# Who makes the low half of each weight chunk, who adds up the last tiles at a norm, and where modulation rows are summed, in a 4-layer fp32 transformer kernel

## The reference, cut to what matters

```python
for l in range(2):                                    # first block
    mod = silu(c) @ w_ada[l] + b_ada[l]               # 9 rows of 1024: sh1, sc1, g1, ...
    y = swiglu(x * (1 + sc1) + sh1, ffn1 weights)     # 1024 -> 2816 -> 1024
    x = layer_norm(ALPHA * x + 0.5 * (1 + g1) * y)
    y = token_mixer(x * (1 + sc2) + sh2)              # w_in, retention/dilated/stick-breaking, w_out
    x = layer_norm(ALPHA * x + (1 + g2) * y)
    y = swiglu(x * (1 + sc3) + sh3, ffn2 weights)
    x = layer_norm(ALPHA * x + 0.5 * (1 + g3) * y)

for i in range(2):                                    # second block
    x = x + mixer_i(rmsnorm(x, g_mix[i]))             # i = 0: even mixer, i = 1: odd mixer
    x = x + cross_attn(rmsnorm(x, g_xattn[i]), rmsnorm(mem, g_mem[i]))
    x = x + square(relu(rmsnorm(x, g_mlp[i]) @ w_up)) @ w_down     # 1024 -> 4096 -> 1024
```

## Time and profile before

| | before |
|---|---|
| median of three runs | 3832.0 us |
| the profiled execution | 3830.17 us, span 3828.9 us |
| TensorE matmuls busy | 3560.9 us, 93% of the span |
| VectorE busy | 1763.9 us, 46% |
| ScalarE busy | 1220.7 us, 32% |
| GpSimd busy | 1426.8 us, 37% |
| mean granted TensorE clock | 0.954 of full speed |

### The profile page before, as it was taken

One profiled execution on the slowest core, in us unless ns is written; L12 is line 12 of the kernel. 1 busy time (PEld: TensorE's weight loads), 2 busy tenths in 40 slices (PEclk: granted clock), 3 DMA queues, 4 the chain that ended last, 5 costly groups with the idle time before them and its releaser, 6 DMA issues.

```text
span 3828.9 us, 41108 instructions
## 1 busy us (share of the span) xinstructions
PE 3560.9 (93%) x16548; PEld 2879.4 (75%) x16548; DVE 1763.9 (46%) x3102; ACT 1220.7 (32%) x1650; POOL 1426.8 (37%) x721
## 2 busy tenths in 40 slices
PE   8999899899998999899799988988989998988999
PEld 7888667688877888667678866746868886777888
DVE  4444654654455444644531235685552224564222
ACT  2222362332223222542332223235342232343222
POOL 3343432333344334322343342212344444525443
PEclk9999899899998999898899989978999998999999
DMA  6333321133342444211122221100212222222222
GB/s 252 143 145 134 107 88 66 72 120 139 143 143 99 143 144 142 99 66 45 65 89 95 92 83 55 56 12 34 89 59 95 99 99 71 98 69 84 91 98 77
DMA packets 52609, 373.42 MB, mean 98 GB/s; under 512 B 5826, under 2 KB 5954, under 8 KB 9539
## 3 DMA queue, kind: packets, MB, share of 16 engines
q1 hardware_dynamic: 52418, 370.79, 26.9%
HBM read 368.67 MB, written 2.10 MB: 97 GB/s over the span
## 4 chain that ended last, share of the span: by engine, by line
PE 82%; DVE 11%; ACT 3%; issue 2%; POOL 2%; DMA 0%; DVEq 0%; ACTq 0%; SPq 0%; POOLq 0%
PE ps L1213 82%; ACT s_wh L1527 1%; DVE s_nu L1808 1%; DVE s_xr L1920 1%; DVE s_tmp L1846 1%; DVE s_tmp L1843 1%; PE ps L1233 0%; ACT s_hh L1527 0%; DVE s_wl L1833 0%; DVE s_tmp L2052 0%; POOL s_hl L2314 0%; ACT s_tmp L1659 0%; DVE s_tmp L2062 0%; POOL s_wl L2321 0%; DVE s_hl L1824 0%
## 5 line engine op out<-in xcount | busy, mean ns | idle before, releaser
L2321 POOL TENSOR_TENSOR s_wl<-s_stage,s_wh 128x1024 fp32r<-128x1024 f32 (+2 forms) x277 | 925.6, 3342 | 1401.3 <-ACT s_wh L1527 1401.0
L1213 PE MATMUL ps<-s_hh,s_wh 128*128 128x512 f32 (+1 forms) x2840 | 1137.8, 401 | 66.8 <-POOL s_hl L2314 45.6
L1213 PE MATMUL ps<-s_hl,s_wh 128*128 128x512 f32 (+1 forms) x2840 | 1119.9, 394 | 0.0
L1213 PE MATMUL ps<-s_hh,s_wl 128*128 128x512 f32 (+1 forms) x2840 | 1118.7, 394 | 0.0
L1527 ACT ACTIVATE s_wh<-s_stage 128x2048 fp32r<-128x2048 f32 (+1 forms) x277 | 519.7, 1876 | 715.3 <-PE ps L1213 684.4
L1213 PEld LDWEIGHTS ps<-s_hh,s_wh 128*128 128x128 f32 (+1 forms) x2840 | 541.4, 191 | 209.2 <-issue 79.0
L1833 DVE TENSOR_TENSOR s_wl<-s_stage,s_wh 128x1024 fp32r<-128x1024 f32 (+1 forms) x268 | 328.2, 1224 | 687.1 <-ACT s_wh L1527 687.1
L1213 PEld LDWEIGHTS ps<-s_hh,s_wl 128*128 128x128 f32 (+1 forms) x2840 | 540.6, 190 | 117.3 <-issue 0.2
L1213 PEld LDWEIGHTS ps<-s_hl,s_wh 128*128 128x128 f32 (+1 forms) x2840 | 541.9, 191 | 112.7 <-issue 2.1
L1213 PE MATMUL ps<-s_ah,s_wh 128*128 128x512 f32 x1216 | 475.3, 391 | 0.0
L1213 PE MATMUL ps<-s_ah,s_wl 128*128 128x512 f32 x1216 | 474.2, 390 | 0.0
(11 more groups left out here) (408 smaller groups left out, 3660.9 us busy)
## 6 DMA issues: line engine op xcount, KB each, us to landing
s_stage<-in_w_ada SPq DMA_DIRECT2D x64, 1024.0 KB, 4.8
s_stage<-in_ffn_w_gate SPq DMA_DIRECT2D x44, 1024.0 KB, 4.8
s_stage<-in_ffn_w_up SPq DMA_DIRECT2D x44, 1024.0 KB, 4.8
s_stage<-in_ffn_down SPq DMA_DIRECT2D x32, 1024.0 KB, 4.8
s_stage<-in_w_up SPq DMA_DIRECT2D x32, 1024.0 KB, 4.8
s_stage<-in_down_m SPq DMA_DIRECT2D x32, 1024.0 KB, 4.8
s_stage<-in_w_in SPq DMA_DIRECT2D x24, 1024.0 KB, 4.8
s_stage<-in_ffn_down SPq DMA_DIRECT2D x16, 768.0 KB, 4.3
```

The costliest lines, as they stand in the source:

```text
L1213: return pe.matmul(out, lhs, rhs, start=start, stop=stop, skip_group_check=True)
L2321: pool.tensor_tensor(m.WL[:, ws, 0:cut], m.STAGE[:, j % NS, 0:cut], m.WH[:, ws, 0:cut].bitcast(F32), ALU.subtract).then_inc(*e.up("pool_w" ...
```

## The change

Four things change together.

1. `split` is only ACT's copy to WH now. A new step `low` has DVE make the whole low half in one instruction, and GpSimd makes none. In `take` it follows the split directly. At a norm the low half of the chunk that `ahead` splits is made inside `ln_b` or `rms_b`, behind tile 5, or at the end of `ln_last`. Where the norm has something else to do meanwhile, as before, nothing is split ahead.
2. The sums of the tiles go on GpSimd only up to tile 5. At a layer norm PE adds tiles 6 and 7 itself: three fp32 matmuls into one bank (the sum of tiles 0 to 5, XR tile 6, XR tile 7) where there was one. At an RMS norm three parts go through the 128x1 matmuls where there was one (the sum of 0 to 5, the squares of 6, the squares of 7). DVE's additions for tile 7 are gone. Of the squares in `ln_a` four folds go to PE (1, 3, 5, 7) where there were three (1, 3, 7), and DVE's two come after all eight subtractions; `ln_last` hands three parts on (3, 5, 7) where it added them into one.
3. In `ln_b` ACT makes HH of the odd tiles (new, L1586 after), GpSimd HL of the odd tiles, and DVE HH and HL of the even ones. In `rms_b` DVE makes the low half of the even tiles and GpSimd that of the odd ones.
4. `ada()` is called at a rate of 0.62 of the chunks taken, where it was every second one; and in the last group's down projection and in `project_out` only the first chunk counts, so that none of the three last chunks before a norm is followed by a modulation row.

The diff, cut to its core:

```diff
-    def split(self, j, whole=False):
+    def split(self, j):
         ws = self.nw % NW
         self.nw += 1
-        self.place[j] = (ws, whole)
-        self.add("split", j, ws, self.stream[j][0], whole, self.wfree[ws])
-        self.staged[j] = [("w.hi", j), ("w.lo", j)] + ([] if whole else [("w.rest", j)])
+        self.place[j] = ws
+        self.add("split", j, ws, self.stream[j][0], self.wfree[ws])
+        self.staged[j] = [("w.lo", j)]
         self.issue(j + NS)
+        return j, ws, self.stream[j][0]
 
     def ahead(self):
+
         i = self.taken + 1
         if self.stream and self.taken < self.nsplit <= i < len(self.stream) and not self.stream[i][2]:
-            self.split(i, True)
             self.nsplit = i + 1
-
-    def take(self, name, idx, raw=False):
+            return self.split(i)
+        return None
+
+    def take(self, name, idx, raw=False, ada=True):
         j = self.taken
         self.taken += 1
         self.order.append((name, idx, raw))
@@ -156,13 +159,13 @@
                 if done > NW - 1:
                     break
                 if i >= self.nsplit:
-                    self.split(i)
+                    self.add("low", *self.split(i))
                     self.nsplit = i + 1
-        self.since += 1
-        if self.every and self.since >= self.every:
-            self.since = 0
+        self.due += self.rate if ada else 0
+        if self.due >= 1:
+            self.due -= 1
             self.ada()
-        return Chunk(j, *self.place.get(j, (0, False)))
+        return Chunk(j, self.place.get(j, 0))
...
                     acc[:] = [self.tmp.take(range(6))]
-                else:
+                elif n < NT - 2:
                     self.add("xsum", sid, n, self.xv[n], self.xv[0], acc[0])
             else:
                 q = self.tmp.take()
-                if n == 0:
-                    acc[:] = [q]
+                if n == 0 or n >= NT - 2:
+                    acc.append(q)
                 self.add("xsq", sid, n, self.xv[n], acc[0], q)
-                if n:
+                if 0 < n < NT - 2:
                     self.tmp.free(q, ("xs", sid, n))
+
+    def squares(self, sid, acc):
+
+        return [(acc[0], ("xs", sid, NT - 3)), (acc[1], ("xq", sid, NT - 2)), (acc[2], ("xq", sid, NT - 1))]
...
-                ch = self.take(names["down"][gi], l * 4 + c)
+                ch = self.take(names["down"][gi], l * 4 + c, ada=gi < len(groups) - 1 or c == 0)
...
-            ch = self.take(name, idx0 + c)
+            ch = self.take(name, idx0 + c, ada=c == 0)
...
-            self.every = 2
+            self.rate = 0.62
...
     def ln_a(l, idx, sid, acc, nxt, xv, s, mean, sq, var):
-        e.wait_ge(("xs", sid, NT - 1), mean.after)
-        mul(m.bank(mean), m.col1024.to_broadcast([P, P]), m.tmp(acc)).then_inc(*e.up("pe_norm", "ln.mean", sid))
+        ones = m.col1024.to_broadcast([P, P])
+        e.wait_ge(("xs", sid, NT - 3), mean.after)
+        mul(m.bank(mean), ones, m.tmp(acc), True, False)
+        for n in (NT - 2, NT - 1):
+            e.wait_ge(xe(n, xv[n]))
+            ins = mul(m.bank(mean), ones, m.XR[:, n, :], False, n == NT - 1)
+        ins.then_inc(*e.up("pe_norm", "ln.mean", sid))
         e.wait_ge(var.after)
-        for i, n in enumerate((1, 3, 7)):
+        for i, n in enumerate((1, 3, 5, 7)):
             e.wait_ge(("ln.fold", sid, n))
-            stat(m.bank(var), 0, 1, m.tmp(sq[n]), m.col1024, i == 0, i == 2).then_inc(*e.up("pe_norm", "ln.var", sid, n))
-
...
-    def rms_a(rid, acc, event, st, y):
-        e.wait_ge(event, st.after)
-        stat(m.bank(st), 0, 1, m.tmp(acc), m.col1024, True, True).then_inc(*e.up("pe_norm", "rms.st", rid))
-
...
             e.wait_ge(("ln.sc", sid, n), qs[n].after)
             act.activation(m.tmp(qs[n]), m.XR[:, n, :], ACT.Identity, bias=B[:, n:n + 1], scale=A[:, n:n + 1]).then_inc(
                 *e.up("act_h", "h.q", hv, n))
+            if n % 2:
+                e.wait_ge(hfree)
+                act.activation(m.HH[:, n, :], m.XR[:, n, :], ACT.Identity, bias=B[:, n:n + 1], scale=A[:, n:n + 1]).then_inc(
+                    *e.up("act_hh", "h.hi", hv, n))
...
-    def split(j, ws, name, whole, wfree):
-        if whole:
-            return
+    def low(j, ws, name):
         n = m.wide(name)
-        cut = n // 2
         e.wait_ge(("w.hi", j))
-        dve.tensor_tensor(m.WL[:, ws, cut:n], m.STAGE[:, j % NS, cut:n], m.WH[:, ws, cut:n].bitcast(F32),
-                          ALU.subtract).then_inc(*e.up("dve_w", "w.rest", j))
+        dve.tensor_tensor(m.WL[:, ws, 0:n], m.STAGE[:, j % NS, 0:n], m.WH[:, ws, 0:n].bitcast(F32),
+                          ALU.subtract).then_inc(*e.up("dve_w", "w.lo", j))
...
                 *e.up("dve_ln", "ln.sub", sid, n))
-            if n >= 6:
-                fold(n - 1)
+        fold(5)
         fold(7)
...
-        for n in range(NT + 1):
-            if n < NT:
-                e.wait_ge(("ln.sq", sid, n))
-                dve.tensor_tensor(m.XR[:, n, :], m.XR[:, n, :], m.bank(rs), ALU.mult).then_inc(
-                    *e.up("dve_ln", "ln.sc", sid, n))
+        for n in range(NT):
+            e.wait_ge(("ln.sq", sid, n))
+            dve.tensor_tensor(m.XR[:, n, :], m.XR[:, n, :], m.bank(rs), ALU.mult).then_inc(*e.up("dve_ln", "ln.sc", sid, n))
+            if n % 2:
+                e.wait_ge(("h.q", hv, n - 1))
+                h_low(hv, n - 1, m.tmp(qs[n - 1]))
+            else:
                 e.wait_ge(("ln.sc", sid, n))
                 dve.tensor_scalar(m.HH[:, n, :], m.XR[:, n, :], A[:, n:n + 1], B[:, n:n + 1], ALU.mult, ALU.add).then_inc(
                     *e.up("dve_hh", "h.hi", hv, n))
-            if n and (n - 1) % 2:
-                e.wait_ge(("h.q", hv, n - 1))
-                h_low(hv, n - 1, m.tmp(qs[n - 1]))
-
-    def ln_last(l, idx, sid, y, var, rs, sq, xv):
+            if n == 5 and low_of:
+                low(*low_of)
...
-            if n >= 6:
-                fold(n - 1)
+        fold(5)
         fold(7)
-        e.wait_ge(("ll.fold", sid, 7), ("ll.fold", sid, 3))
-        dve.tensor_tensor(m.tmp(sq[7]), m.tmp(sq[7]), m.tmp(sq[3]), ALU.add).then_inc(*e.up("dve_fold", "ll.fold", sid, 8))
-
-    def rms_a(rid, acc, event, st, y):
+        if low_of:
+            low(*low_of)
...
             if n % 2:
-                h_low(hv, n, m.tmp(qs[n]))
+                h_low(hv, n - 1, m.tmp(qs[n - 1]))
+            if n == 5 and low_of:
+                low(*low_of)
...
-    def split(j, ws, name, whole, wfree):
-        n = m.wide(name)
-        cut = n if whole else n // 2
-        e.wait_ge(("w.hi", j))
-        pool.tensor_tensor(m.WL[:, ws, 0:cut], m.STAGE[:, j % NS, 0:cut], m.WH[:, ws, 0:cut].bitcast(F32),
-                           ALU.subtract).then_inc(*e.up("pool_w", "w.lo", j))
-
...
-        elif n < NT - 1:
+        else:
...
-        for n in range(0, NT, 2):
+    def ln_b(sid, y, var, rs, s, hfree, hv, qs, low_of):
+        for n in range(1, NT, 2):
             e.wait_ge(("h.q", hv, n))
```

More of the change, by code:

```diff
@@ L222, in ada_first @@
         if self.stream:
-            self.split(0)
+            self.add("low", *self.split(0))
             self.nsplit = 1
@@ L329, in layer_norm @@
         self.banks.free(mean, ("ln.sub", sid, NT - 1))
-        for n in (1, 3, 7):
+        for n in (1, 3, 5, 7):
             self.tmp.free(sq[n], ("ln.var", sid, n))
-        self.ahead()
+        low = self.ahead()
         y, rs = self.yr.take(), self.banks.take()
@@ L336, in layer_norm @@
             self.hv += 1
-            self.add("ln_b", sid, y, var, rs, s, self.hfree, self.hv, self.to_h())
+            self.add("ln_b", sid, y, var, rs, s, self.hfree, self.hv, self.to_h(), low)
             self.banks.free(rs, ("ln.sc", sid, NT - 1))
@@ L357, in layer_norm @@
         self.small.free(s, ("ln.sub", sid, NT - 1))
-        return sid, [sq[7]], ("ll.fold", sid, 8)
+        return [(sq[n], ("ll.fold", sid, n)) for n in (3, 5, 7)]
     def rms_norm(self, name, l, total, meanwhile=None):
-        sid, acc, event = total
-        rid = self.new()
+        rid, low = self.new(), None
         st, y = self.held.take(), self.yr.take()
-        self.add("rms_a", rid, acc[0], event, st, y)
-        self.tmp.free(acc[0], ("rms.st", rid))
+        self.add("rms_a", rid, total, st, y)
+        for q, _ in total:
+            self.tmp.free(q, ("rms.st", rid))
         self.held.free(st, ("rs.v", rid))
@@ L2357, in ln_last, with rms_b @@
                 *e.up("pool_sum", "ll.fold", sid, n))
-    def rms_b(rid, name, l, y, b, qs, xv, hfree, hv):
-        for n in range(0, NT, 2):
+    def rms_b(rid, name, l, y, b, qs, xv, hfree, hv, low_of):
+        for n in range(1, NT, 2):
             h_low(hv, n, m.tmp(qs[n]))
@@ L2426, in gpsimd @@
     run(plan, dict(
-        split=split, mod_first=mod_first, xsum=xsum, xsq=xsq, ln_a=ln_a, ln_b=ln_b, ln_last=ln_last, rms_b=rms_b,
```

(1 more changed line is left out.)

75 lines of the change are left out of this document (35 added, 40 removed).

## The result

The changed kernel takes 3772.05 us (median of four runs, 3767.59 to 3776.20), the kernel before 3830.93 us in the runs beside it; the ratio is 0.9844, with a 95% interval of 0.9827 to 0.9861. The profiled execution has a span of 3766.3 us, 62.6 less than before.

A forecast was written before the change was run, and what follows sets the result against it. PE was taken to set the time between norms, so the change counts at twelve norms. Terms sum to -32.6 from 3830.2 us, giving 3797.6, and 3799 with the median 1.8 above; stated range 3776 to 3822.

The forecast's parts named there:

- The root: Root of the variance: L1808 falls to 0.17 us without GpSimd's weight half, -20 at six layer norms, -12 at three RMS norms.
- the +1.2 taken: Layer norm statistics: a fourth part through PE at half clock, 7.5 us instead of 5.6, +1.2 a norm, six times +7.
- Rival 1: Clock stays full through the statistics: four parts take 4.2 instead of 7.5 us, -17, total 3783; chance 0.15.
- RMS norms: Three RMS norms: root -12, statistics -1 over three, first tile of h -0.65 each, -2; forecast -15 in the table.
- The third norm: Behind the third norm, nothing split ahead: a new wait of about 7 us on a weight half, +8 (bounds 0 and +12).
- In the other mixers ... 0, bounds -3 and +8: Other mixers: DVE has more to do, about +1.1 us for each of 277 chunks, GpSimd less; net 0, bounds -3 and +8.
- -2 for the cross attentions: Two cross attentions: PE waits for a whole DVE half of 2.35 us instead of GpSimd's 3.43, -1.1 each, -2.
- the -13 at the means: Mean of the layer norms: modulation rows moved three chunks earlier, 3.96 us at norms 1 and 4, 4.9 at 3, 0.3 at 2.
- 300 us: Sign in the profile after: DVE busy up by about 300 us (277 x 1.1) from its longer low halves.
- Rival 3: L1808's 3.5 us are its own, GpSimd has nothing to do with it: the 32 us are not there, 3831; chance 0.05.
- Rival 2: Stalls behind the norms grow through DVE's long low halves and the third norm's wait: +16 to +28, 3815 to 3827; chance 0.10.
- Rival 4: Mixers and cross attentions: DVE becomes the late engine for weights, 81 chunks x 1.1 = +87, 3885, slower; chance 0.06.

The follow-up runs named there:

- the doubled half: The changed kernel with DVE's low-half instruction issued two times for each weight chunk, one after the other; 3875.1 us in one run, +103.

## Why the prediction was wrong

Its steps at the norms held. The root: L1808 fell to 0.17 us everywhere. Statistics: from mean to root it was 9.1 us in all six norms and is 9.5 to 10.5, so +1.0 a norm on the mean for the +1.2 taken. Four parts at half clock take 6.99 us, not 7.5. Rival 1 (clock stays full) has a small part in that: in norms 1 and 5 the granted clock is 0.50 and the parts take 6.99 and 6.96 us, but in the other four the first matmuls of the statistics still run at full clock (mean 0.56 to 0.64) and the parts take 6.10 to 6.45 us. Its 4.2 us came nowhere. RMS norms: -5.4 for -5.0 each. The third norm: a wait of 6.15 us for "about 7", and +8.8 for +8. Norms 1 to 5 gave -27.7 for -26.

The step that failed is the term for the stretches between the norms, "In the other mixers ... 0, bounds -3 and +8", together with -2 for the cross attentions. In place of 0 the table shows about -21: the mixer of layer 1, the stretch behind norm 5, and the even and the odd mixer lie 24 us below their forecasts, the other stretches 3 above. In place of -2 it shows -6.7. Behind the first stands what rows of modulation cost in a mixer, a price that the sum did not have.

- The chain showed two L1843 at 3.78 us, and I took that as the price of modulation rows. It was the same waiting for GpSimd as in L1808: 0.35 us each when GpSimd is quiet. I had the rule and did not ask which other DVE instructions it slows. So DVE's work didn't rise by 300 us, it stayed. And the -13 at the means, booked to moving the rows, can be had from either part: the low half alone brings the mean of norm 1 to 3.08 us behind the projection with the rows unmoved, moving the rows alone brings it to 3.81. With the low half made, moving the rows adds nothing there. The term's size was right; that it belongs to the rows alone was wrong, and that both causes give it only once was luck.
- In the mixer of layer 1 the new rate leaves no rows. I priced moved rows only by what stood before norms, and took what they leave as hidden. The experiments put their absence at 6 to 14 us in that stretch, where 13 us of the miss lie. This is the largest piece of it. The order of instructions told that all rows are done before this mixer; I had not carried it into the sum.
- Cross attention: I priced the weight half, -1.1 each, by the chain's 3.43 us. PE itself stood only 0.21 us there, so little of it could show. What shrank is the norm of k, which I hadn't looked at. It has an L1808 and an L1816 that wait for GpSimd. DVE's timeline there before, then PE's before, with the low half alone, and after:

```profile
2729.72 2.18 DVE L1808 TENSOR_SCALAR s_nu<-s_nv 128x4 int32<-128x4 int32 x1
...
2735.37 2.24 DVE L1816 SCALAR_TENSOR_TENSOR s_nu<-s_na,s_nv 128x4 f32<-128x4 f32 x1
...
2733.92 1.16 PE L1213 MATMUL ps<-s_cc,s_ny 128*128 128x128 f32 x8 [2.01 <-DVE s_ny L1819]
2734.84 0.44 PE L1213 MATMUL ps<-s_wh,s_mh 128*128 128x256 f32 x1
```

```profile
2696.43 1.85 PE L1221 MATMUL ps<-s_cc,s_ny 128*128 128x128 f32 x8 [2.27 <-DVE s_ny L1827]
```

```profile
2693.94 1.10 PE L1215 MATMUL ps<-s_cc,s_ny 128*128 128x128 f32 x8
2694.79 0.36 PE L1215 MATMUL ps<-s_wh,s_mh 128*128 128x256 f32 x1
```

PE waited 2.0 us and then ran its next matmuls of 256 columns at 0.42 us; after, there is no wait and they take 0.28: -3.7 and -3.0. But the waiting for GpSimd is not what this was worth. With the low half alone L1808's 2.18 us are gone, yet PE waits 2.27: DVE's whole half, 2.29 us long, stands before the chain instead, and the norm of k takes 13.5 us both times, where it took 13.2 and 12.5. With all but the low half it takes 10.4, with both 9.5. So most of the gain comes from parts 2 and 3 of the change (sums of the tiles, roles in making h); which of the two was not separated.

- Behind norm 5, -4.7 for +2. The low half alone gives -6.5 there, without it the stretch is 372.6. PE's wait for a small DVE chain (3.34 us before) is 1.74 after, and another went from 1.6 to 0.5. The rest of it is not located.

Rival 3 (L1808's time is its own) is out. Rival 2 was right in its place (third norm, tile 5) but not in its size. Rival 4 did not come, and the doubled half shows how far off it was. Its sum has a slip: 81 times 1.1 is 89, not 87. The range failed because all bounds were set around norms, and the mixers' side below zero was put at 3 us with no row behind it.
